# Layer 1 of a two-layer backbone step: the residual is stored to the sum rows ahead of the expert tiles, and the outputs are copied from there within DRAM

## What is computed

```python
        xp = xp + mod_p[2] * mp
        xs = xs + mod_s[2] * ms
        mo = (m_w_gr[layer], m_b_gr[layer], m_w_er[layer], m_b_er[layer],
              m_w_gate[layer], m_w_up[layer], m_w_down[layer])
        xp = xp + mod_p[5] * hier_moe(modulate(rms_norm(xp, g_norm2[layer]), mod_p[3], mod_p[4]), *mo)
        xs = xs + mod_s[5] * hier_moe(modulate(rms_norm(xs, g_norm2[layer]), mod_s[3], mod_s[4]), *mo)
    return (xp, xs, jnp.stack(new_ckv, 1), jnp.stack(new_krope, 1), jnp.stack(new_sf, 1), jnp.stack(new_sb, 1))
```

## Time and profile before

| | us |
|---|---|
| median of 3 runs | 1632.24 |
| the runs | 1630.11 to 1633.37 |
| span of the profiled execution, first to last instruction | 1625.3 |
| PE busy in it | 1466.2 (90%) |
| DVE busy | 814.1 (50%) |
| ACT busy | 477.5 (29%) |
| POOL busy | 201.1 (12%) |

### The profile page before, as it was taken

The page is one execution under the profiler, slowest core; times in us unless marked ns, Lnnn a source line. Parts: engine busy times, 40 slices in busy tenths (PEclk is TensorE's granted clock), DMA queues, the critical chain, the costliest instruction groups (busy, mean ns, idle before and its releaser), DMA issues.

```text
span 1625.3 us, 33987 instructions
## 1 busy us (share of the span) xinstructions
PE 1466.2 (90%) x14700; PEld 1041.6 (64%) x14700; DVE 814.1 (50%) x1573; ACT 477.5 (29%) x1066; POOL 201.1 (12%) x201
## 2 busy tenths in 40 slices
PE   3999889999999999788999988989988999999993
PEld 2555467774568888455766767767755445688882
DVE  1356775662544343344655665665653625443433
ACT  2200653430300000164554554555422203000000
POOL 2200020010121211111110110110100002222211
PEclk9999989999999999898999998999999999999997
DMA  9674275644299999532111021012010433899985
GB/s 347 249 271 138 79 240 168 225 148 166 93 315 336 350 337 293 141 90 60 29 56 44 23 63 44 22 45 76 5 58 26 168 134 106 279 342 338 345 261 168
DMA packets 165557, 271.28 MB, mean 167 GB/s; under 512 B 7504, under 2 KB 107088, under 8 KB 164768
## 3 DMA queue, kind: packets, MB, share of 16 engines
q1 hardware_dynamic: 149568, 206.29, 37.7%
q0 software_dynamic: 15840, 62.83, 13.3%
HBM read 240.06 MB, written 36.36 MB: 170 GB/s over the span
## 4 chain that ended last, share of the span: by engine, by line
PE 65%; DVE 10%; issue 5%; ACT 4%; DMA 2%; DVEq 2%; POOL 0%; POOLq 0%; ACTq 0%; SPq 0%; PEldq 0%
PE psum L1601 14%; PE psum L873 8%; PE psum L2037 8%; PE psum L1612 7%; PE psum L2099 4%; PE psum L908 3%; PE psum L2049 2%; PE psum L2592 2%; PE psum L1593 2%; PE psum L887 2%; PE psum L1323 2%; PE psum L311 2%; PE psum L898 1%; DVE modN L2409 1%; PE psum L2186 1%
## 5 line engine op out<-in xcount | busy, mean ns | idle before, releaser
L2037 PE MATMUL psum<-hT,ring 128*128 128x384 f32 (+1 forms) x736 | 244.0, 457 | 0.7 <-ACTq L212 0.7
L2037 PEld LDWEIGHTS psum<-hT,ring 128*128 128x128 f32 x736 | 129.6, 196 | 34.6 <-issue 2.7
L1601 PEld LDWEIGHTS psum<-arena,ring 128*128 128x128 f32 x1152 | 131.1, 192 | 12.0 <-issue 10.0
L1601 PE MATMUL psum<-arena,ring 128*128 128x128 f32 x1152 | 132.0, 276 | 4.4 <-DVE arena L1635 4.4
L1673 DVE TENSOR_TENSOR arena<-arena,psum 128x256 f32<-128x256 f32 x34 | 14.3, 421 | 211.6 <-PE psum L1601 211.6
L708 DVE SCALAR_TENSOR_TENSOR arena<-arena,params_sb 128x655 f32<-128x655 f32 x120 | 106.0, 910 | 4.8
L2099 PEld LDWEIGHTS psum<-arena 32*32 32x32 f32 x5120 | 55.4, 111 | 65.7 <-issue 38.4
L2099 PE MATMUL psum<-arena 32*32 32x32 f32 x5120 | 64.2, 200 | 27.7 <-issue 17.2
L1545 POOL DMA_INDIRECT ysum<-arena,small x34 | 53.9, 1584 | 285.4 <-DVE arena L1643 284.8
L1656 ACT ACTIVATE arena<-psum 128x256 f32<-128x256 f32 x34 | 13.0, 383 | 222.3 <-PE psum L1601 222.3
L553 PE MATMUL psum<-hT,ring 128*128 128x512 f32 (+1 forms) x256 | 72.1, 438 | 0.7 <-ACT modN L423 0.7
(11 more groups left out here) (467 smaller groups left out, 2641.6 us busy)
## 6 DMA issues: line engine op xcount, KB each, us to landing
ring<-in_w_mod SPq DMA_DIRECT2D x24, 1024.0 KB, 5.1
ring<-in_m_w_gate SPq DMA_DIRECT2D x18, 1024.0 KB, 13.2
ring<-in_m_w_up SPq DMA_DIRECT2D x18, 1024.0 KB, 17.2
ring<-in_m_w_down SPq DMA_DIRECT2D x18, 1024.0 KB, 14.7
arena<-in_w_mod SPq DMA_DIRECT2D x16, 1024.0 KB, 5.1
modN<-in_m_w_down SPq DMA_DIRECT2D x16, 1024.0 KB, 16.0
ring<-in_c_w_in SPq DMA_DIRECT2D x24, 512.0 KB, 6.1
arena<-in_m_w_gate SPq DMA_DIRECT2D x8, 1024.0 KB, 13.5
```

The source lines that it names most:

```text
L1601: m = pe.matmul(bank((2, 4)[half] + (1, 3)[half] * q, P, f * P), gu_slot[s][:, c0:c0 + P], xgT[:, q, k, :], start=(k == 0), stop=(k == KC ...
L2037: m = pe.matmul(bank(un % 2, w), ring[:, s, c0k:c0k + P], hT[:, k, o:o + w], start=(k == 0), stop=(k == KC - 1))
```

## The change

1. `clear_sums` no longer zeroes the 640 token rows of `ysum[1]`; its 256 pad rows are still zeroed, and so is all of `ysum[0]`. Three DRAM-to-DRAM copies fewer.
2. In `moe_sp` for layer 1, after the load of the gate/up weights of expert 0, SP waits for each `out_x` and stores the tile of `X` to its rows of `ysum[1]`: five stores of 0.5 MB. The scatters then add the expert results on top of the residual.
3. POOL's wait ahead of the first gather of layer 1 is on those five stores (`moe1_base`, 80) instead of on the zeroing. In layer 0 the wait is unchanged.
4. `comb1_act`, `comb1_dve` and the call of `comb_sp(sp, 1)` are gone. A new `outputs_sp` waits for POOL's end of `moe1` and copies the rows of `ysum[1]` to the outputs in five DRAM-to-DRAM copies on SP's queue.

```diff
         def clear_sums(pool, l):
-            for r in range(0, T, NPAD):
-                rows = min(NPAD, T - r)
-                pool.dma_start(ysum[l][r:r + rows, :], h2d[T:T + rows, :]).then_inc(S(f"moe{l}_cleared"), 16)
+            if l == 0:
+                for r in range(0, T, NPAD):
+                    rows = min(NPAD, T - r)
+                    pool.dma_start(ysum[l][r:r + rows, :], h2d[T:T + rows, :]).then_inc(S(f"moe{l}_cleared"), 16)
             pool.dma_start(ysum[l][T:T + NPAD, :], h2d[T:T + NPAD, :]).then_inc(S(f"moe{l}_cleared"), 16)
...
                 gate_up_of(0, 0)
+                for t in range(NT):
+                    sp.wait_ge(S("out_x"), NT + t + 1)
+                    sp.dma_start(ysum[1][t * P:(t + 1) * P, :], X[:, t, :]).then_inc(S("moe1_base"), 16)
             sp.wait_ge(S("norm_h"), (2 * l + 2) * NT)
...
-            count_wait(pool, "moe1_cleared", 64)
+            if l == 0:
+                count_wait(pool, "moe1_cleared", 16)
+            else:
+                count_wait(pool, "moe1_base", 16 * NT)
...
-        def comb1_dve(dve):
-            dve.wait_ge(S("side_loads"), 160)
-            for t in range(NT):
-                comb_add(dve, 1, t)
-            barrier(dve, "dve", "comb1")
+        def outputs_sp(sp):
+            sp.wait_ge(S("pool_phase_done"), phase_no["moe1"])
+            sp.dma_start(O["y_prompt"][0], ysum[1][0:P, :]).then_inc(S("y_out"), 16)
+            for t in range(1, NT):
+                sp.dma_start(O["y_sample"][0, (t - 1) * P:t * P, :], ysum[1][t * P:(t + 1) * P, :]).then_inc(S("y_out"), 16)
+            sp.wait_ge(S("y_out"), 16 * NT)
...
             moe_sp(sp, 1)
-            comb_sp(sp, 1)
-            for t in range(NT):
-                sp.wait_ge(S("cb_used"), NT + t + 1)
-                dst = O["y_prompt"][0] if t == 0 else O["y_sample"][0, (t - 1) * P:t * P, :]
-                sp.dma_start(dst, X[:, t, :]).then_inc(S("y_out"), 16)
-            sp.wait_ge(S("y_out"), 16 * NT)
+            outputs_sp(sp)
```

More of the change, by code:

```diff
@@ L122, in build_program @@
                  "moe1_dn_w2": ("z1_w0", 16), "moe1_dn_w3": ("z1_w1", 16),
-                 "moe0_cleared": ("pad_stored", 32), "moe1_cleared": ("pad_stored", 96), "moe1_x0": ("pad_stored", 160), "moe1_x1": ("small_loaded", 48), "moe1_x2": ("mod_bias", 256),
+                 "moe0_cleared": ("pad_stored", 32), "moe1_cleared": ("pad_stored", 96), "moe1_x0": ("pad_stored", 112), "moe1_base": ("rest_loaded", 32), "moe1_x1": ("small_loaded", 48), "moe1_x2": ("mod_bias", 256),
                  "moe1_x3": ("mod_stored", 128), "moe1_scattered0": ("mod_bc", 64),
@@ L216, in barrier @@
                     eng.wait_ge(S(f"{other}_phase_done"), n)
-        for name in ["norm0a", "in0", "attn0", "moe0", "norm1a", "gates1", "heads1", "z1", "moe1", "comb1"]:
+        for name in ["norm0a", "in0", "attn0", "moe0", "norm1a", "gates1", "heads1", "z1", "moe1"]:
             phase_no[name] = len(phase_no) + 1
@@ L1775, in comb0_pool @@
             pool.memset(UU, 0.0)
-        def comb1_act(act):
-            barrier(act, "act", "comb1")
-        def comb1_dve(dve):
-            dve.wait_ge(S("side_loads"), 160)
-            for t in range(NT):
-                comb_add(dve, 1, t)
-            barrier(dve, "dve", "comb1")
+        def outputs_sp(sp):
[4 more added lines that the diff above has]
+            sp.wait_ge(S("y_out"), 16 * NT)
         G0 = 100
@@ L2697, in _ @@
             moe_act(act, 1)
-            comb1_act(act)
         @block.vector
@@ L2714, in _ @@
             moe_dve(dve, 1)
-            comb1_dve(dve)
         @block.gpsimd
```

## The result

| | before | after |
|---|---|---|
| median of 6 runs each | 1631.17 | 1620.15 |
| the runs | 1626.70 to 1637.07 | 1615.03 to 1623.34 |
| span of the profiled execution | 1625.3 | 1613.1 |

The ratio is 0.9933, 95% interval 0.9914 to 0.9951: the changed kernel is 0.7% faster, 11.0 us by the medians. Three further comparisons of the same two kernels gave 0.9931, 0.9924 and 0.9932. The forecast was 1623.6 us with a range of 1620.5 to 1628.6. The direction and the three places were right.

What follows compares the result with a forecast made beforehand. PE was taken to bound the chain (65%), with DMA mattering only where engines wait and at the byte-bound end. Minus 6.5 (end), minus 2.6 (start), plus 0.5 (gather) took 1632.24 to 1623.6 us, range 1620.5 to 1628.6.

Steps and rivals of the forecast that it cites:

- The wait goes whole: 2.6 us: Early `w_mod` load: with three zeroing copies fewer it lands before PE asks, saving 2.6 us (0 to 2.6).
- the end of the down weights for 1.2 us: Layer 1's first gather: shares DMA with the last down-weight bytes at half rate; +0.6 less 0.2 slack, +0.5 us.
- Copies at half rate: End: reads and writes share one limit, 213 GB/s, so the gain is 1.7 us, giving 1628.4 us; chance 0.13.
- The early wait only moves: Start: DVE's convolution work sets that stage's end, so the 2.6 us reappear as a wait, 1626.2 us; chance 0.12.
- The gather waits for the stores: Layer 1's first gather: residual stores land late, at 1398.8, costing +3.6 instead of +0.5, 1626.7 us; chance 0.10.
- Few engines carry the copies: End: SP's queue spreads copies over 4 of 16 DMA engines, 87 GB/s, a loss at 1646.1 us; chance 0.04.
- The 6.94 us between span and median: Whole kernel: a fixed 6.94 us was added to the forecast span of 1616.7 to get 1623.6 us.

Runs made afterwards that it cites:

- experiment with two queues: Changed kernel with output copies of tiles 0, 2, 4 issued by SP and 1, 3 by ACT: ratios 0.9911 and 0.9916 to the kernel before.
- small rows: Changed kernel with output copies in rows of 4 KB instead of 32 KB: end 11.2 us, where the changed kernel takes 11.2, 12.1, 11.1 and 10.8.
- doubled stores: Changed kernel with the five residual stores repeated to a spare DRAM tensor: stretch at layer 1's first gather 6.40 us longer than in the first trace of before.
- the start alone: Kernel before with only layer 1's three early zeroing copies moved from 73 us to about 1295 us: ratios 0.9978 and 0.9976 to the kernel before.

## Why the prediction was right, and where it was off

**The mechanism held at all three places, the range did not.** The wait for `w_mod` is gone and nothing took its place; the gather is still released by DVE; the end is a single pass of the bytes. The signs that the prediction named are in the trace of after: no wait near 102, the load landed at 97.2 (about 97 forecast) after 6.8 us (5 to 7), DVE as releaser, about 10 us of end (11.2). The gather's 4.2 us lie just under the 4.4 to 5.4 named.

**The step that failed is the start.** "The wait goes whole: 2.6 us", with bounds of 0 and 2.6. The upper bound was the wait of one execution. Measured over six traces the early copies cost 4.1 us, between 2.7 and 6.1, and the kernels that only move them are 3.6 and 3.9 us faster, with intervals that don't tell these from 2.6. Two things were missing: the wait varies (2.58 to 3.25), and in three of six traces the granted clock fell to 0.5 behind it. The earlier trace rows are one of the three without, so nothing in the first trace showed it. It is 1.5 us of the 3.45 by which the time undercut the forecast, the largest part that a term explains; 1.1 us are only the level of the runs before, which is luck. With an upper bound of 6.1 the low end of the range would have held the time. The other end was added up wrong: the sum of the bounds is 1621.1 to 1630.9 (1632.24 - 4.9 + 3.6), not to about 1627. The measured time lies at the low end, so this did no harm. On why it is only some executions the Trainium skill has a sentence: page "TensorE: Matmul & The Clock Gate", section "Part 1: The HAM clock gate", says that the gate's windows run free of the kernel, so that the same kernel can meet them differently in each run. The traces agree as far as they go, three of six, and one of three of before itself; they can't show the gate.

**The end was put 1 us too high.** The forecast was 10.2 us in place of 16.7, a gain of 6.5 (4.9 to 8.5). Measured are 11.2, 12.1, 11.1, 10.8, 11.6, 11.5 and 10.7 us with copies on one queue, in the mean 11.3, against 16.7, 17.9, 16.7, 16.6 and 16.3 without, in the mean 16.8. The gain is 5.5 us. The forecast took 7.5 us for the bytes, at the rate of engines that are all busy, and 2.7 us for the rest. In after the bytes took 9.0 us from first to last, and the rest is 2.2 us: 1.4 us ahead of the first byte and 0.8 us behind the last. The rate was not the mistake: at 370 GB/s, reckoned as in the earlier trace rows, the bytes would have taken 7.1 us. The mistake was to count on full engines for copies that start up and run out within 9 us: the share over them was 0.78. The experiment with two queues got 0.3 to 0.6 us of this back, the small rows nothing.

**The stores cost nothing instead of 0.5.** The forecast had the gather meet "the end of the down weights for 1.2 us". It met nothing: in after SP's queue was done at 1391.1 at the latest, which is 1397.7 on the clock of before, where the forecast had 1398.8, and the gather's bytes began behind it. What was mis-sized is the rate: 338 GB/s was read in a window that holds the accumulating store too, while the stretch from 1373.2 to 1378, without it, ran at 421 GB/s. At that rate 2.62 MB are 6.2 us of work and not 7.8. The last store landed at 1383.6, 6.1 us ahead of the gather's issue, where the forecast had 3.6. With and without stores the stretch at the gather is the same to 0.1 us in the mean. The doubled stores show what a collision costs where PE has to wait for it: 6 us.

**The rivals.** *Copies at half rate* falls: 291 GB/s on SP's queue from first to last byte, where half rate was 213. By the figure of the page "DMA: Bandwidth & Descriptors" of the Trainium skill, section "Latency and other measured facts", the bytes would have taken 12.2 us, an estimate; they took 9.0, and the measurement decides. That figure is for tiles whose rows lie 512 KiB and more apart, and these copies are contiguous. *The early wait only moves* falls by the start alone: the stretches behind it keep their length. *The gather waits for the stores* falls by its releaser. *Few engines carry the copies* falls by the share of 0.78 over 9.1 us.

**The 6.94 us between span and median were not fixed.** Every later execution has its device time and its span from the same run, and they are 1.9 to 2.6 us apart (after: 1615.03 and 1613.1). So the first trace of before was an execution of about 1627.3 us, 4 us faster than the median of 1631.17. This made no difference to the forecast, since both sides of it carried the same 6.94. But it was the sign that the trace was a favourable draw, and with it the wait in the earlier trace rows.

**The sum.** 4.1 + 5.5 + 0 = 9.6 us by traces (or 9.5 with 0.1 for the stores), against 11.0 by the medians, whose interval is 8.0 to 14.0 us (0.9951 and 0.9914 of 1631). The two agree within it. Against the forecast of 1623.6 the 3.45 us are 1.1 from the level of the runs before (1631.17 for 1632.24), 1.0 from the three terms (+1.5 at the start, -1.0 at the end, +0.5 at the stores), and 1.4 that no term takes up. All four comparisons lie on the same side of 9.6. The granted clock, listed with each run, goes some way to name this rest. In 117 runs of before and 31 of after, the time within one kernel falls by 1.1 us for each 0.001 of clock (correlation -0.84). The runs of after had 0.9642 in the mean, those of before 0.9609. Of the 0.0033 between them some 0.0017 is the shorter end, where the clock stands at 0.50, and some 0.0009 the spell at the start (2.9 us at 0.50 in the mean of the six traces). The last 0.0007 would be worth 0.8 us, an estimate from these runs. With it the terms make 10.4 us, and the means of these runs differ by 11.1, with an interval of some 1.7 either way. So part of the rest sits in spells at low clock in stages that the change does not touch. Whether the change shifts these, or chance did, no run shows.

## What to carry to other kernels

A wait of PE read in one trace is one draw, and its price is the wait plus what the clock does behind it: bound it by several traces, or above by more than the bracket says. Before two windows of two traces are compared, line them up by an instruction that both have. And where runs differ by more than the terms explain, look at the granted clock of each run first. Background copies without any reader are free only until a load that someone waits for is queued with them, so put them where the DMA engines are idle and no load is near its time. A pass through SBUF at the end of a program costs its bytes twice, and if the sum can be collected in DRAM, a copy costs them once.

## What the runs showed of the hardware

- The granted clock fell from 1.00 to 0.50 behind a wait of PE of 2.6 to 3.3 us in three of six executions, and stayed at 1.00 in the other three, for waits of 2.6 to 2.9 us. The length of the wait doesn't sort them: 2.58 had the drop and 2.85 had not. The 16 matmuls behind it took 7.9 to 9.1 us instead of 7.1. Over 148 runs of before and after, the time of one kernel moves by 1.1 us for 0.001 of mean granted clock.
- Five DRAM-to-DRAM copies of 0.5 MB ran at 291 GB/s from first to last byte on SP's queue. Per busy time of the DMA engines it is 370 GB/s, and 349 GB/s for the larger ones on POOL's queue. Rows of 4 KB instead of 32 KB raised the share from 0.84 to 1.00 in 7 us and lowered the rate per share from 379 to 343 GB/s, so the end took as long.
- Of the 11.2 us of such an end, 1.4 pass before the first byte and 0.8 behind the last. Issuing the copies from two engines took 0.3 to 0.6 us off.
- While POOL's queue moved 7.34 MB of copies in rows of 64 KB (87.5% of the DMA engines' time), SP's queue with three loads waiting moved 0.59 MB (8.6%).
- A gather of 0.5 MB landed in 4.2 us when SP's queue had run dry ahead of its first byte, though it was still busy at the issue. It landed in 7.8 us beside a queue that was not done; the wait of 3.09 us that this made cost PE 5.8 us with the clock.
